# Keys and queries projected first, values last, the normalised input made beside the value tiles, and the squares taken from GpSimd to ScalarE and VectorE

## What is computed

```python
def rms_norm(x, g):
    y = xf * lax.rsqrt(jnp.mean(xf * xf, axis=-1, keepdims=True) + NORM_EPS)
    return (y * g.astype(jnp.float32)).astype(x.dtype)

def project_layer(x, pos, norm_g, w_in):
    h = rms_norm(x, norm_g) @ w_in
    pr = dict(zip(IN_NAMES, jnp.split(h, IN_OFFSETS, axis=-1)))
    q_a = rope(pr['q_a'].reshape(b, t, N_DIL * A_HEADS, HEAD_DIM), pos)
    k_a = rope(pr['k_a'].reshape(b, t, N_DIL * A_KV, HEAD_DIM), pos)
    q_c = rope(pr['q_c'].reshape(b, t, C_HEADS, HEAD_DIM), pos)
    kv_c = pr['kv_c'].reshape(b, t, 6, C_KV, HEAD_DIM)
    ...
    # 5 key tiles, 5 value tiles, 2 tiles of raw rows to compress, 16 query tiles of 128 columns each;
    # then the gates z_a, z_b, z_c, the inputs of the convolution, g_c and g_merge
```

## Time and profile before

| | us |
|---|---|
| median of 3 runs | 1024.5 (1018.6, 1024.5, 1024.67) |
| profiled execution | 1019.13 |
| its span | 1017.5 |
| TensorE busy | 956.3 (94%) |
| VectorE busy | 597.2 (59%) |
| ScalarE busy | 422.4 (42%) |
| GpSimd busy | 200.0 (20%) |

### The profile page before, as it was taken

The page is one execution under the profiler, slowest core; times in us unless marked ns, Lnnn a source line. Parts: engine busy times, 40 slices in busy tenths (PEclk is TensorE's granted clock), DMA queues, the critical chain, the costliest instruction groups (busy, mean ns, idle before and its releaser), DMA issues. The chain is left out here.

```text
span 1017.5 us, 21063 instructions
## 1 busy us (share of the span) xinstructions
PE 956.3 (94%) x7878; PEld 869.7 (85%) x7878; DVE 597.2 (59%) x1324; ACT 422.4 (42%) x835; POOL 200.0 (20%) x334
## 2 busy tenths in 40 slices
PE   6999888998999999999999998999989999999996
PEld 6999777887778689999999987888877776999996
DVE  6878476557222357646667857666661224675564
ACT  4543445544312254344453544454542204443443
POOL 8000000125437620000000000003273474000000
PEclk9999999999999999999999999999999999999999
DMA  9563954526658882532645575537347698633521
GB/s 350 212 254 128 398 210 187 227 115 208 229 156 253 264 313 67 220 128 104 239 186 224 226 307 196 191 151 291 117 145 231 200 277 260 260 125 125 205 85 47
DMA packets 65477, 206.30 MB, mean 203 GB/s; under 512 B 12112, under 2 KB 49680, under 8 KB 56032
## 3 DMA queue, kind: packets, MB, share of 16 engines
q1 hardware_dynamic: 56480, 185.31, 49.2%
q0 software_dynamic: 8752, 19.63, 6.4%
q10 hardware_dynamic: 144, 0.01, 0.0%
HBM read 200.12 MB, written 40.18 MB: 236 GB/s over the span
## 5 line engine op out<-in xcount | busy, mean ns | idle before, releaser
L1650 DVE TENSOR_TENSOR big_r<-big,paged_r 128x1024 fp32r<-128x1024 f32 x160 | 195.5, 1231 | 129.4 <-ACT paged_r L1434 128.7
L985 PE MATMUL bank<-xnT_high_r,paged_r 128*128 128x288 f32 x768 | 232.7, 303 | 7.5 <-DVE sgt L1877 3.4
L985 PE MATMUL bank<-xnT_r,paged_r 128*128 128x288 f32 x704 | 208.7, 296 | 0.0
L985 PE MATMUL bank<-xnT_high_r,big_r 128*128 128x288 f32 x704 | 208.1, 296 | 0.0
L985 PE MATMUL bank<-short_r,big_r 128*128 128x288 f32 x576 | 171.2, 297 | 0.0
L1434 ACT ACTIVATE paged_r<-big 128x1024 fp32r<-128x1024 f32 x160 | 166.4, 1051 | 6.2 <-DMA big<-in_w_feat 4.2
L985 PEld LDWEIGHTS bank<-xnT_high_r,paged_r 128*128 128x128 f32 x768 | 144.9, 189 | 15.4 <-issue 7.8
L985 PE MATMUL bank<-short_r,paged_r 128*128 128x288 f32 x448 | 134.5, 300 | 12.4 <-DVE big_r L1650 10.1
L985 PE MATMUL bank<-kvp_r,paged_r 128*128 128x288 f32 x448 | 134.0, 299 | 0.0
L985 PEld LDWEIGHTS bank<-xnT_high_r,big_r 128*128 128x128 f32 x704 | 133.3, 189 | 0.0
L985 PEld LDWEIGHTS bank<-xnT_r,paged_r 128*128 128x128 f32 x704 | 133.1, 189 | 0.0
(11 more groups left out here) (313 smaller groups left out, 1484.5 us busy)
## 6 DMA issues: line engine op xcount, KB each, us to landing
big<-in_w_tok SPq DMA_DIRECT2D x13, 2048.0 KB, 8.7
big<-in_w_feat SPq DMA_DIRECT2D x12, 2048.0 KB, 8.5
big<-in_w_gate SPq DMA_DIRECT2D x10, 2048.0 KB, 9.1
out_kept_dil<-in_cache_dil SPq DMA_DIRECT2D x16, 1020.0 KB, 13.2
paged<-in_pool SPq DMA_DIRECT2D x218, 64.0 KB, 3.0
big<-in_w_up SPq DMA_DIRECT2D x12, 1024.0 KB, 9.5
paged<-in_pool POOLq DMA_DIRECT2D x166, 64.0 KB, 2.9
big<-in_kv_win SPq DMA_DIRECT2D x4, 2048.0 KB, 8.9
```

The lines of the kernel that those rows point to most:

```text
L985: last = mm(out, l, r, start=(c == 0 and i == 0), stop=(c == n - 1 and i == 2))
L1650: v.tensor_tensor(l_part, full, h_part.bitcast(FP32), ALU.subtract).then_inc(*split_done.inc(s))
```

## The change

1. TILES: keys (5), raw rows (2), queries (16), values (5), where it was values (4), keys (5), raw rows (2), one value tile, queries (16). So i = 0 to 4 are keys, 5 and 6 raw rows, 7 to 22 queries, 23 to 27 values. The raw queries of the four groups stand in three buffers in turn, and ScalarE's copy of a group waits for the rotation that last used its buffer (RAW_AFTER).
2. Group q 3 is turned in one piece, in step 22; so all four query rotations stand in the projection (steps 10, 14, 18, 22), and none in the units.
3. The norm steps move: norm(z) from steps 4 to 6 and 13 to 14 (layer 0; 1 to 3 in layer 1) to step z + 19, nlow(z) to step z + 20.
4. root becomes one product of a 128x128 matrix of ones with the summed squares (128x288), followed by a square root on ScalarE and a reciprocal of 128x288 on VectorE; spread falls away within the layers; a step rnt turns the factor of 288 tokens into three columns, for the values. At the end of the program root and spread stay as they were. root stands in step 2 of layer 0 (it was 3) and 0 of layer 1.
5. In layer 0 the squares are ScalarE's and their sum VectorE's, four of them in step 0 and four in step 1. GpSimd starts its constants as soon as the last quarter of the first weights has landed.
6. SyncE waits for the second piece of x before it starts the third and the fourth.
7. vturn and gc are written in another order, gct comes after the first score, and the gates za stand ahead of zc.

```diff
-TILES = [("v", t) for t in ("d1", "d4", "d16", "win")] + [("k", t) for t in KEYED[0:4]] + \
-        [("k", "slc"), ("cmp", 0), ("cmp", 1), ("v", "slc")] + [("q", t, r) for t in range(4) for r in range(REP)]
+TILES = [("k", t) for t in KEYED] + [("cmp", 0), ("cmp", 1)] + [("q", t, r) for t in range(4) for r in range(REP)] + \
+        [("v", t) for t in KEYED]
 V_SLC = TILES.index(("v", "slc"))
-K_FIRST, K_SLC = TILES.index(("k", "d1")), TILES.index(("k", "slc"))
+V_FIRST, K_SLC = TILES.index(("v", "d1")), TILES.index(("k", "slc"))
+
+RAW_AFTER = {("q", 2, 0): ("k", 0), ("q", 3, 0): ("q", 0), ("v", "d1"): ("q", 1), ("v", "slc"): ("k", 1)}
 
 ROPES = {TILES.index(("k", "win")): ("k", 0), K_SLC: ("k", 1)} | \
         {TILES.index(("q", t, REP - 1)): ("q", t) for t in range(4)}
...
-        root, first = (0, 1) if layer else (3, 4)
+        if layer == 0 and i < 2:
+            out += [("square", 4 * i + z) for z in range(4)]
+        root = 0 if layer else 2
         if i == root:
-            out.append(("root",))
-        elif i == first:
-            out += [("spread",), ("rots",), ("norm", 0), ("norm", 1)]
-        elif first < i < first + 3:
-            n = 2 * (i - first)
-            out += [("nlow", n - 2), ("nlow", n - 1), ("norm", n), ("norm", n + 1)]
-        elif i == first + 3:
-            out += [("nlow", 4), ("nlow", 5)]
-        elif 12 < i < 16:
-            out += [("nlow", z) for z in range(6, KT) if z == i - 8] + [("norm", z) for z in range(6, KT) if z == i - 7]
+            out += [("root",), ("rots",)]
+        elif i == root + 2:
+            out.append(("rnt",))
+        out += [("nlow", z) for z in range(KT) if z == i - 20] + [("norm", z) for z in range(KT) if z == i - 19]
         if i < 12:
             pass
         elif i < 14:
             out += tile_splits(2 * i - 10, 2 * i - 9)
         elif i + 4 < len(TILES) + 2:
             out += tile_splits(i + 4)
-        if i in ROPES and ROPES[i] != ("q", 3):
+        if i in ROPES:
             out.append(("rope",) + ROPES[i])
         if i == TILES.index(("cmp", 1)):
             out.append(("pairs",))
-    out += [("gc",)] + [("vturn", j) for j in range(4)] + [("gct",)]
+    out += [("vturn", 1), ("vturn", 2), ("gc",), ("vturn", 3), ("vturn", 0)]
...
+        if i == 0:
+            out.append(("gct",))
...
-        if i < 2:
-            out.append(("rope", "q", 3, i))
...
-    raw_k = [oT[1][:, 0:4, :], oT[0][:, 0:1, :]]
-    raw_q = [oT[1], oT[0], oT[1], oT[0]]
+    raw_q = [oT[0], oT[2], oT[1], oT[0]]
...
             load_x(1)
             load_first(0)
+            sp.wait_ge(x_in[1], 16)
             load_x(2)
...
+            pool.wait_ge(first_in[3], 16)
+            for dst, src in LATE:
+                pool.dma_start(dst, src).then_inc(late_in, 16)
+            numbers = page_numbers(pool, 0)
...
+                    pe.wait_ge(set_up, 4)
+                    wait(pe, TR.is_free(s))
+                    if layer < DEPTH:
+                        pe.wait_ge(*summed.at(("square", KT - 1)))
+                        mm(tr(s)[:, 0:T], ones[:, :], total[:, 0:T], start=True, stop=True).then_inc(*TR.fill(s))
+                        continue
...
+                elif k == "rnt":
+                    pe.wait_ge(*inverted.at(("root",)))
+                    pe.wait_ge(const_in, 16 * len(CONSTS))
+                    transposes(s, [(tr(s)[0:PARTS[tt], tt:tt + 1], rnB[0:1, TOK0[tt]:TOK0[tt] + PARTS[tt]])
+                                   for tt in range(3)])
...
+                    dst, src = (rnB, tr(s)[:, 0:T]) if layer < DEPTH else (rn, tr(s)[:, 0:3])
+                    f(dst, src, ACT.Sqrt, bias=eps, scale=1.0 / D_MODEL).then_inc(*TR.release(s))
+                elif k == "rnt":
                     act.wait_ge(*TR.is_full(s))
-                    f(rnB, tr(s)[:, 0:T], ACT.Copy).then_inc(*TR.release(s))
+                    f(rn[:, 0:2], tr(s)[:, 0:2], ACT.Copy)
+                    f(rn[0:NS, 2:3], tr(s)[0:NS, 2:3], ACT.Copy).then_inc(*TR.release(s))
...
-                    if kind == "q" and q4 == 0:
-                        act.wait_ge(*roped.at((("k", 0), ("k", 1), ("q", 0), ("q", 1))[g - 3]))
-                    dst = raw_q[g - 3][:, q4, :] if kind == "q" else prod[:, :] if i == V_SLC else \
-                        raw_v[:, q4, :] if kind == "v" else raw_k[i // K_SLC][:, q4, :]
+                    if TILES[i] in RAW_AFTER:
+                        act.wait_ge(*roped.at(RAW_AFTER[TILES[i]]))
+                    dst = raw_q[TILES[i][1]][:, TILES[i][2], :] if kind == "q" else raw_k[i // K_SLC][:, i % K_SLC, :] \
+                        if kind == "k" else prod[:, :] if i == V_SLC else raw_v[:, i - V_FIRST, :]
                     f(dst, pj(s)[:, 0:T], ACT.Copy, scale=SCALE if kind == "q" else 1.0).then_inc(*PJ.release(s))
...
+                    if layer < DEPTH:
+                        v.reciprocal(rnB, rnB).then_inc(*inverted.inc(s))
+                        dve.wait_ge(*inverted.at(s))
+                        continue
...
```

More of the change, by code:

```diff
@@ L191, in prompt_units @@
     return [(br, qt, r) for br in "AC" for qt in range(2) for r in range(REP)]
-FEATS = [("zc", kt) for kt in range(WT)] + [("za", kt) for kt in range(WT)] + \
+FEATS = [("za", kt) for kt in range(WT)] + [("zc", kt) for kt in range(WT)] + \
         [(kind, kt) for kt in range(WT) for kind in ("h", "c", "b", "zb")]
@@ L354, in start @@
 def start(layer, i):
-    return [(layer, ("start", i)), (layer, ("square", i))]
+    return [(layer, ("start", i))] + [(layer, ("square", i))] * (layer > 0)
 def program_steps():
@@ L503, in trunk_program @@
     prod = sb("prod", [P, T])
+    raw_k = [oT[1][:, 0:4, :], prod[:, :].unsqueeze(1)]
     w2 = sb("w2", [P, 2, HD])
@@ L541, in trunk_program @@
             pj_keys.append((layer, s[0:4]))
-        if k in ("root", "spread", "vturn", "gct", "ghidt", "cturn", "cmpt", "sturn", "sgateA", "sgateC"):
+        if k in ("root", "rnt", "spread", "vturn", "gct", "ghidt", "cturn", "cmpt", "sturn", "sgateA", "sgateC"):
             tr_keys.append((layer, s))
@@ L918, in _ @@
                 k = s[0]
[L919 to L935 removed]
+                if s == ("rope", "k", 1):
                     pool.wait_ge(*roped.at(("k", 1)))
@@ L1050, in _ @@
                     j = s[1]
-                    for i in [V_SLC] if j == 0 else range(2, 4):
+                    for i in [V_SLC] if j == 0 else range(V_FIRST + 2, V_FIRST + 4):
                         pe.wait_ge(*PJ.is_used(("proj", i)))
@@ L1376, in _ @@
                       scale=gT[:, layer, i:i + 1]).then_inc(*x_rounded.inc(s))
-                elif k == "square" and layer:
+                elif k == "square":
                     i = s[1]
@@ L1600, in _ @@
                         .then_inc(*x_split.inc(s))
-                elif k == "square" and layer:
+                elif k == "square":
                     i = s[1]
-                    if i == 0:
+                    if layer == DEPTH and i == 0:
                         v.memset(total[:, T:3 * P], 1.0)
                         v.memset(squared_x[1][:, T:3 * P], 0.0)
-                    if i == KT - 1:
+                    if (layer, i) == (DEPTH, KT - 1):
                         continue
@@ L1624, in _ @@
                 elif k == "rots":
-                    dve.wait_ge(*TR.is_used(("spread",)))
+                    if layer == 0:
+                        dve.wait_ge(const_in, 16 * len(CONSTS))
                     v.tensor_tensor(rot_n[:, 0, :], rot_c[:, :], rnB, ALU.mult)
@@ L1659, in _ @@
                 elif k == "rope":
[L1660 removed]
+                    kind, t = s[1:]
                     i = next(j for j in ROPES if ROPES[j] == (kind, t))
[L1662 to L1663 removed]
+                    for j in {max(i - 1, 0), i}:
                         dve.wait_ge(*PJ.is_used(("proj", j)))
[L1665 removed]
                     if s[1:] != ROPED[0]:
[L1667 to L1675 removed]
+                        dve.wait_ge(*roped.at(ROPED[ROPED.index(s[1:]) - 1]))
+                    source = raw_q[t][:, :, :] if kind == "q" else raw_k[t]
+                    part, turned = turn_pairs(source, swapped[:, 0:source.shape[1], :])
                     if kind == "k":
@@ L1687, in _ @@
                             out = qblk[rows, t, :, :].rearrange("p h (b k r t) -> p (h b) k r t", b=RB, k=KV, r=REP)
-                            last = v.tensor_tensor(out[:, :, kv, reps, :], new, new_turned, ALU.add)
+                            last = v.tensor_tensor(out[:, :, kv, :, :], new, new_turned, ALU.add)
                     last.then_inc(*roped.inc(s[1:]))
```

66 lines of the change are left out of this document (10 added, 56 removed).

## The result

| | before | the change |
|---|---|---|
| median, us | 1022.93 (4 runs, 1018.6 to 1024.67) | 1033.17 (4 runs, 1032.54 to 1034.08) |
| profiled execution, us | 1019.13 | 1032.55 |
| its span, us | 1017.5 | 1030.9 |

The ratio of the change to before is 1.0107, with a 95% interval of 1.0071 to 1.0144: slower by 1%. The profiled executions differ by 13.4 us, where 11.7 was forecast. The profiled execution of before lies 3.8 under the median of its runs, that of the change 0.6 under its own; so the medians differ by only 10.2. The kernel before was run again beside the experiments, 42 times in all, with medians of 1020.1 to 1021.3; against these the change costs 12 to 13 us, near what the two traces show.

What follows compares the result with a forecast made beforehand. TensorE, busy 956.3 of 1017.5 us, was taken as the bound, so new stalls are paid in full. Layer 0 +6.5, layer 1 +5.5, clock -0.3 sum to +11.7; forecast 1033.5, between 1030.8 and 1036.2, range 1020 to 1042.

Steps and rivals of the forecast that it cites:

- item 4: Steps 19 to 27: ScalarE's copies stand behind waits for VectorE; stalls of 1.4 and 6.2, +9.6 us per layer.
- item 6: TensorE's clock: -1.5 us in layer 1's first units, +0.6 per layer behind the long wait at tile 26; net -0.3.
- item 1: Start of layer 0: TensorE begins 1.2 us earlier, given back by later root and squares; zero, from -1.8 to +3.
- Rival E: Start of layer 0: the constants delay tok1's load, +3 us, 1036.5; chance 0.06.
- item 3: q 0 in step 10: tile 13's split stands behind this rotation, +1.4 us per layer.
- item 2: root and spread: -0.7 us in layer 1; a new reciprocal of 2.2 delays layer 0's key rotation, +0.3.
- item 5: The units: gaps behind q 3's half rotations go, -4.8 us per layer.
- Rival C: The units: the gaps aren't the rotation's, so up to 9.6 us isn't won, 1043; chance 0.08.
- Rivals A and B: A: copies never stall TensorE, 1011.3, chance 0.06; B: round trips catch up before q 3, about 1022, chance 0.12.
- D: Clock falls after each long stall and stays down through the last tiles and gc: 1038; chance 0.10.

Runs made afterwards that it cites:

- Experiments 3 and 4: The change with ScalarE rounding each normalised slice one step later: 1013.91 us; the change with norms 4 to 7 in steps 12, 13, 16, 17: 1013.58 us.
- experiment 7: The change plus 40 idle TensorE products of 128x288 ahead of tile 26: 1034.2 us, ratio 1.0134 to the kernel before.
- experiment 6: Two variants of the change, one execution each: GpSimd's constants started after tok1's load, 1033.08 us; SyncE not waiting for x, 1028.75 us.
- experiment 8: The change with weights prepared four tiles ahead from step 6 and rotations k 0, k 1, q 0 in steps 7, 8, 11: 1030.15 us.
- experiment 2: The change with q 3 turned in two halves in units 0 and 1 again, gates zc ahead of za: 1041.6 us, ratio 1.0177.

## Why the prediction was right, and where its terms were off

**The main term (item 4): +9.6 forecast, +9.50 and +9.51 measured.** The waits were to be 1.4 and 6.2, and are 1.18 and 5.95; the round trip was to be 3.48, and is; gc was to start 40.5 after the end of tile 18, and starts 40.57 and 40.59 after it. ScalarE stood 5.39 and 7.71, where about 6 was expected both times. Experiments 3 and 4 show the cause as stated: ScalarE's copy behind a wait for VectorE. What was wrong is the 0.6 per layer that item 6 added for the clock behind the long wait. Tile 26 lost 2.4 us to it in layer 0, and gc then had no wait left; in layer 1 it lost 1.8, and gc waited 0.54; with the clock kept up (experiment 7) gc waited 1.71. It starts at the same place each time, when the last low part is there, so the clock added nothing.

**The start (item 1): 0 forecast, +3.0 measured, at the edge of the range given for it (-1.8 to +3). This is the term that was mis-sized.** TensorE did start earlier (8.42, 1.7 before), and the four products of x took 1.80 us together instead of 3.70. But tok1's load came 1.5 us later than the row from which I had it, the sums ended at 25.0 instead of 23.0, and I had not counted that a wait of 5.3 us is followed by a tile at the lower clock (0.24 us from one matmul to the next, about 1.6 in all). The step that failed: item 1 took from SyncE's wait for x only its gain, and left the loads behind it where they were, though they stand behind it in SyncE's list. tok1's load starts 1.8 later (11.52 for 9.69), and without the wait (experiment 6, one execution) tile 5 starts at 30.89, 0.2 earlier than before the change, which is the zero of the forecast. (19.79 itself is no sure arrival: that row shows no wait for the load, only that it was in by then.) Rival E named the constants as the cause; experiment 6 shows no effect of them. The +3 at the start that it priced came, but from another cause; that the range held it is luck.

**q 0 in step 10 (item 3): +1.4 forecast, 1.41 measured,** and gone in experiment 8.

**root and spread (item 2): -0.7 forecast, about -1.2 measured** (+0.25 in tiles of layer 1, less 1.4 for q 0). The 0.3 for the key rotation in layer 0 didn't come: the gap at tile 6 is 0.60 there, where the kernel before had 1.03 behind its key rotation. The reciprocal took 1.95 us, where the slope of the earlier trace rows gave 2.2. The estimate from the repeat count that the Trainium skill names (VectorE: DVE Perf Modes, First, the fixed hardware budget) was 2.4. The flat 0.45 is ruled out; both estimates were too high, by 0.25 and 0.45.

**The units (item 5): -4.8 forecast, -5.16 measured;** experiment 2 brought the gaps back. Rival C is out.

**The clock (item 6): -1.5 in layer 1 came true** (6.68 won there, 5.16 in layer 0). Not forecast: 1.74 in layer 0's later stretch, at granted 0.98. It lies behind a wait of 2.7 us for ScalarE that the kernel before has as well, at full clock in its profiled execution. The Trainium skill (TensorE: Matmul & The Clock Gate, Part 1) has idleness bring the throttle back; the trace agrees at tile 26, with granted 0.50 behind 5.95 us of standing still.

Rivals A and B are out by the two waits. D is out by the trace of the change: tile 27 and gc run at full clock, and the stretch that holds them costs no more than item 4 had. The sum of the terms was 11.7 and is 13.4, and that it is so close is in part luck: the start and the later stretch came 4.7 over, the rest 3.0 under (1.4 in the two main stretches, of which 1.2 is the clock that cost nothing; 0.7 in the units; 0.4 and 0.5 in the tiles ahead). That the forecast of 1033.5 came within 0.4 of the median owes something to the base too, for I had put it between the profiled execution and the median.

## What to carry to other kernels

When work is moved on an engine that frees a shared buffer, don't ask how busy the engine is but what stands ahead of the freeing copy in its order: a wait for another engine there hands that engine's longest piece on to whoever needs the buffer. Put the waiting instruction behind the next copy, which here cost nothing and gave back 1.9% of the time; then look for the next wait where the reader arrives earlier than before. A list of loads is such an order too: a wait put into it moves every load behind it. And before you price the removal of a stall, see whether a wait of another cause follows it: slow clock and idle time ahead of that wait are not paid twice.

## What the runs showed of the hardware

- A TensorE that had stood still for 10 us ran its first tile in 5.93 us; with products of ones in that time it took 3.21. (In the other kernels without such products it took 4.7 to 5.9.) The window's granted clock reads 1.00 for both, so at the start of an execution the spacing of the matmuls (0.24 or 0.13 us) is the sign to go by.
- Behind the same wait of 1.71 us (experiment 7), the next product ran at granted 0.55 in one layer and at full clock in the other.
- A reciprocal over 128x288 took 1.95 us on VectorE, against 0.46 for a product of the same shape.
- The same start lets the first matmul begin anywhere between 8.42 and 9.56 us, by when the first weights land. A single profiled execution fixes such a term only to about 1 us.
